# Folding the partition halves of the modulation sums on VectorE, and half as many matmuls to sum them on TensorE

## What is computed

```
mod_lat = (jax.nn.silu(c) @ w_mod[layer] + b_mod[layer])[:, None, :]
mod_ctx = (jax.nn.silu(c_ctx) @ w_mod[layer] + b_mod[layer])[None, None, :]
ml = jnp.split(mod_lat, N_MOD, axis=-1)
mc = jnp.split(mod_ctx, N_MOD, axis=-1)
x = x + 0.5 * ml[2] * swiglu(modulate(rms_norm(x, norm1_g[layer]), ml[0], ml[1]),
                              ffn1_w_in[layer], ffn1_w_out[layer])
```

## Time and profile before

| | |
|---|---|
| runs, median of 3 | 1243.94 us (1243.44 to 1244.24) |
| the profiled execution, span from the first to the last instruction | 1242.0 us |
| TensorE busy | 1226.1 us (99%), 7268 matmul passes |
| VectorE busy | 911.0 us (73%) |
| ScalarE busy | 591.5 us (48%) |
| GpSimd busy | 57.0 us (5%) |
| DMA | 214.22 MB, mean 172 GB/s |

### The profile page before, as it was taken

How to read it: one execution, slowest core, us unless ns; L and a number is a source line. 1 busy time by engine, 2 the same in 40 slices (tenths; PEclk the granted TensorE clock), 3 DMA queues, 4 the chain that set the end, 5 groups by cost and what they waited for, 6 DMA issues and landing times.

```text
span 1242.0 us, 19650 instructions
## 1 busy us (share of the span) xinstructions
PE 1226.1 (99%) x7268; PEld 1054.4 (85%) x7268; DVE 911.0 (73%) x1438; ACT 591.5 (48%) x917; POOL 57.0 (5%) x65
## 2 busy tenths in 40 slices
PE   8999999999999999999999999999999999999998
PEld 6788888888888798788888888889798999888887
DVE  3887877778657676788787776667769977667765
ACT  3632222222325546655555655546475576554552
POOL 2000000000002000000001000000012301000001
PEclk9999999999999999999999999999999999999999
DMA  9665544555422244323454565554533334455542
GB/s 387 233 241 203 203 169 172 201 203 199 145 73 94 102 170 169 136 102 106 167 202 170 188 227 194 189 183 167 208 135 116 123 133 173 170 182 208 185 170 102
DMA packets 31826, 214.22 MB, mean 172 GB/s; under 512 B 3472, under 2 KB 4752, under 8 KB 7056
## 3 DMA queue, kind: packets, MB, share of 16 engines
q1 hardware_dynamic: 31184, 211.83, 47.1%
q10 hardware_dynamic: 576, 1.48, 0.3%
HBM read 212.24 MB, written 1.05 MB: 172 GB/s over the span
## 4 chain that ended last, share of the span: by engine, by line
PE 91%; DVE 4%; DMA 2%; ACT 1%; issue 1%; SPq 0%; DVEq 0%; ACTq 0%
PE ps_u L1960 27%; PE ps_u L1969 14%; PE ps_u L1970 14%; PE ps_u L1971 14%; PE ps_u L1962 13%; DMA scr<-in_mods 1%; DVE w_lo L1081 1%; PE ps_a L1884 1%; PE ps_a L2219 1%; DMA raw<-in_stream 1%; PE ps_a L2203 1%; PE ps_a L1941 1%; PE ps_a L2413 0%; PE ps_a L1930 0%; ACT w_hi L553 0%
## 5 line engine op out<-in xcount | busy, mean ns | idle before, releaser
L553 ACT ACTIVATE w_hi<-raw 128x1024 fp32r<-128x1024 f32 x322 | 339.0, 1056 | 294.5 <-PE ps_u L1971 170.8
L1081 DVE TENSOR_TENSOR w_lo<-raw,w_hi 128x1024 fp32r<-128x1024 f32 x322 | 393.6, 1224 | 93.0 <-ACT w_hi L553 92.2
L1969 PE MATMUL ps_u<-x_hi,w_hi 128*128 128x512 f32 (+1 forms) x768 | 263.5, 343 | 2.8 <-DVE x_lo L1257 1.6
L1971 PE MATMUL ps_u<-x_hi,w_lo 128*128 128x512 f32 (+1 forms) x768 | 258.0, 336 | 0.0
L1960 PE MATMUL ps_u<-x_hi,w_hi 128*128 128x512 f32 x720 | 229.0, 399 | 0.4 <-DVE x_hi L1167 0.4
L1970 PE MATMUL ps_u<-x_lo,w_hi 128*128 128x512 f32 (+1 forms) x624 | 217.5, 349 | 0.0
L1969 PEld LDWEIGHTS ps_u<-x_hi,w_hi 128*128 128x128 f32 x768 | 145.6, 190 | 25.1 <-issue 6.9
L1962 PEld LDWEIGHTS ps_u<-x_hi,w_lo 128*128 128x128 f32 x720 | 135.2, 188 | 31.9
L1971 PEld LDWEIGHTS ps_u<-x_hi,w_lo 128*128 128x128 f32 x768 | 145.6, 190 | 15.3
L1962 PE MATMUL ps_u<-x_hi,w_lo 128*128 128x256 f32 x720 | 141.6, 278 | 0.0
L1960 PE MATMUL ps_u<-h_hi,w_hi 128*128 128x512 f32 x432 | 141.1, 396 | 0.0
(11 more groups left out here) (336 smaller groups left out, 1519.0 us busy)
## 6 DMA issues: line engine op xcount, KB each, us to landing
raw<-in_stream SPq DMA_DIRECT2D x153, 1024.0 KB, 4.8
wide_scr<-in_mods SPq DMA_DIRECT2D x18, 1024.0 KB, 7.0
scr<-in_mods SPq DMA_DIRECT2D x18, 1024.0 KB, 7.0
raw<-in_stream SPq DMA_DIRECT2D x8, 768.0 KB, 4.2
x<-in_tokens SPq DMA_DIRECT2D x2, 1024.0 KB, 6.5
wide_scr<-in_cmp_w SPq DMA_DIRECT2D x8, 256.0 KB, 5.1
sq<-in_cmp_w SPq DMA_DIRECT2D x2, 1024.0 KB, 6.1
out<-x SPq DMA_DIRECT2D x4, 256.0 KB, 2.2
```

Source lines behind the costliest of these rows:

```text
L553: act.activation(w_hi[:, k % 2, cols], raw[:, k % 2, cols], ACT.Copy).then_inc(h_ready, 1)
L1081: dve.tensor_tensor(w_lo[:, k % 2, cols], raw[:, k % 2, cols], w_hi[:, k % 2, cols].bitcast(F32), ALU.subtract).then_inc(l_ready, 1)
L1969: pe.matmul(dst, wh, xh, start=(kc == 0), stop=False)
L1971: ins = pe.matmul(dst, wl, xh, start=False, stop=(kc == span - 1))
```

## The change

`mod_sums` tiles are folded before TensorE sees them. Behind the last quarter of a chunk VectorE adds, for vector 0, partitions 64 to 127 of its tile to partitions 0 to 63, in place; then, when that is done, for vector 1 the halves of its tile, into partitions 64 to 127 of vector 0's tile. Each add counts the new semaphore `mod_folded`. `mod_sum` waits for two of them per chunk in place of the sixteen counts of `mod_added`, and takes that one tile with a new stationary operand `half_cols` (column 0 is ones on the lower half, column 1 on the upper): four matmuls in place of eight, none of them accumulating.

`half_cols` needs three more memsets on VectorE in front; `ones_ready` counts to 9 in place of 6. The two row-statistics semaphores of k and q become one (`head_rows`), so do their roots (`head_roots`) and q's reciprocal and scale (`q_scale_steps`); each wait stands where it stood.

```diff
+HALF_ROWS = P // 2
+        half_cols = sb("half_cols", [P, MOD_ROWS])
+        mod_folded = sem("mod_halves_folded")
...
-        kstat_rows = sem("kstat_rows_done")
+        head_rows = sem("k_then_q_stat_rows_done")
-        qstat_rows = sem("qstat_rows_done")
...
-            act.wait_ge(qstat_rows, 1)
+            act.wait_ge(head_rows, 2)
...
+            dve.memset(half_cols[:], 0.0).then_inc(ones_ready, 1)
             dve.memset(tick[:], 0.0).then_inc(o1_done, 1)
             dve.memset(vc_tok[:], 0.0).then_inc(ones_ready, 1)
-            dve.wait_ge(ones_ready, 4)
+            dve.wait_ge(ones_ready, 5)
+            for v in range(2):
+                dve.memset(half_cols[v * HALF_ROWS:(v + 1) * HALF_ROWS, v:v + 1], 1.0).then_inc(ones_ready, 1)
...
                         ins.then_inc(mod_added, 1)
+                if quarter == MOD_QUARTERS - 1:
+                    low, high = slice(0, HALF_ROWS), slice(HALF_ROWS, P)
+                    for v, rows in enumerate((low, high)):
+                        total_v = mod_sums[:, chunk % 2, v, :]
+                        dve.wait_ge(mod_added, 4 * n + 3 + v)
+                        if v:
+                            dve.wait_ge(mod_folded, 2 * chunk + 1)
+                        dve.tensor_tensor(mod_sums[rows, chunk % 2, 0, :], total_v[low, :], total_v[high, :], ALU.add)\
+                           .then_inc(mod_folded, 1)
...
             def mod_sum(c):
 
-                pe.wait_ge(mod_added, 4 * MOD_QUARTERS * (c + 1))
+                pe.wait_ge(mod_folded, 2 * (c + 1))
                 pe.wait_ge(mod_turned, c if c >= 3 else 2)
-                for v in range(2):
-                    for g in range(P // MOD_ROWS):
-                        rows = slice(g * MOD_ROWS, (g + 1) * MOD_ROWS)
-                        ins = pe.matmul(ps_a[rows, MOD_BANKS[c], 0:MOD_COLS], one_col[:, v, :],
-                                        mod_sums[:, c % 2, v, g * MOD_COLS:(g + 1) * MOD_COLS], start=(v == 0), stop=(v == 1))
+                for g in range(P // MOD_ROWS):
+                    rows = slice(g * MOD_ROWS, (g + 1) * MOD_ROWS)
+                    ins = pe.matmul(ps_a[rows, MOD_BANKS[c], 0:MOD_COLS], half_cols[:],
+                                    mod_sums[:, c % 2, 0, g * MOD_COLS:(g + 1) * MOD_COLS], start=True, stop=True)
                 ins.then_inc(mod_summed, 1)
...
-            pe.wait_ge(ones_ready, 6)
+            pe.wait_ge(ones_ready, 9)
```

More of the change, by code:

```diff
@@ L309, in program @@
         kstat_done = sem("kstat_done")
-        kroot_done = sem("kroot_done")
+        head_roots = sem("k_then_q_roots_done")
         krecip_done = sem("krecip_done")
@@ L321, in program @@
         qstat_done = sem("qstat_done")
-        qroot_done = sem("qroot_done")
-        qrecip_done = sem("qrecip_done")
-        q_scaled = sem("q_scale_ready")
+        q_scale_steps = sem("q_scale_steps")
         q_swapped = sem("q_swapped")
@@ L774, in _ @@
             act.wait_ge(kstat_done, 1)
-            act.activation(root[:, 0:8], ps_a[:, 1, 8:16], ACT.Sqrt, bias=eps, scale=1.0 / HD).then_inc(kroot_done, 1)
+            act.activation(root[:, 0:8], ps_a[:, 1, 8:16], ACT.Sqrt, bias=eps, scale=1.0 / HD).then_inc(head_roots, 1)
             with act.Fori(0, 2) as p:
@@ L805, in _ @@
             act.wait_ge(qstat_done, 1)
-            act.activation(root[:, 16:32], ps_a[:, 1, 16:32], ACT.Sqrt, bias=eps, scale=1.0 / HD).then_inc(qroot_done, 1)
+            act.activation(root[:, 16:32], ps_a[:, 1, 16:32], ACT.Sqrt, bias=eps, scale=1.0 / HD).then_inc(head_roots, 1)
             with act.Fori(2, 4) as p:
@@ L1437, in _ @@
             dve.drain().then_inc(drained, 1)
-            dve.wait_ge(kstat_rows, 1)
+            dve.wait_ge(head_rows, 1)
             dve.tensor_copy(k_stat_parts, ps_a[:, 1, S:NB]).then_inc(kstat_copied, 1)
@@ L1442, in _ @@
             split(0, k + 3, 1)
-            dve.wait_ge(kroot_done, 1)
+            dve.wait_ge(head_roots, 1)
             dve.reciprocal(rstd[:, 0:8], root[:, 0:8]).then_inc(krecip_done, 1)
@@ L1493, in _ @@
                     dve.tensor_tensor(q_rows[:, h, :], t1[:, j, 0:S], t1[:, j, S:NB], ALU.add).then_inc(drained, 1)
[L1496 to L1502, removed]
+            dve.wait_ge(head_roots, 2)
+            dve.reciprocal(rstd[:, 16:32], root[:, 16:32]).then_inc(q_scale_steps, 1)
+            dve.wait_ge(q_scale_steps, 1)
+            dve.tensor_scalar(q_scale[:], rstd[:, 16:32], float(HD) ** -0.5, None, ALU.mult).then_inc(q_scale_steps, 1)
+            dve.wait_ge(q_scale_steps, 2)
             def turned1(h, b=3):
@@ L2129, in _ @@
                                     start=True, stop=True)
-            ins.then_inc(kstat_rows, 1)
+            ins.then_inc(head_rows, 1)
             def k_stat(kc):
@@ L2152, in q_stat_rows @@
                                             start=(v == 0), stop=(v == 1))
-                    ins.then_inc(qstat_rows, 1)
+                    ins.then_inc(head_rows, 1)
             def q_stat(kc):
@@ L2192, in _ @@
                     gates(p, j)
-            pe.wait_ge(qroot_done, 1)
+            pe.wait_ge(head_roots, 2)
             pe.wait_ge(v_ready, 2)
```

## The result

The kernel after takes 1247.31 us (median of 15 runs, 1245.97 to 1248.93) beside 1244.2 us for the kernel before (15 runs, 1243.42 to 1244.48): a ratio of 1.0026, 95% interval 1.0019 to 1.0032. It is 3.1 us slower, a little past the 0.2% that can be told from no change. The prediction, 1245.5 us, has the sign and about half of the size (1.6 of 3.1 us); its range, 1243.0 to 1248.6, holds the time.

A forecast was written before the change was run, and what follows sets the result against it. TensorE, busy 99% of the span, was taken to bound the kernel. Waits of 4.66 us less 3.02 saved gave +1.64, so 1243.9 + 1.6 = 1245.5 us, range 1243.0 to 1248.6.

The forecast's parts named there:

- What is removed: TensorE's mod_sum: two sets of four passes fewer, 0.43 us per chunk, 3.0 us in all, all on the path.
- What is added: VectorE: two adds per chunk behind its last product, 1.22 us each, each starting 0.03 us after the instruction before.
- When TensorE gets its sums: Sums may begin 2.57 us after the products; TensorE waits in five of seven chunks, 4.66 us in all.
- The sum of the stage: First feed-forward stage: waits of 4.66 us less 3.02 saved, +1.64 us.
- The lateness is not carried on: VectorE's 2.6 us of lateness go into its idle time and cost nothing; the rival, +15 us, had chance 0.05.
- What lies around the span: The 1.9 us between the profiled span and the median of the runs was taken as unchanged.
- The rest at nothing: The three extra memsets in front, the merged k and q semaphores and TensorE's clock under new waits cost nothing.
- the forecast's own case: The whole kernel at 1244.4 to 1246.7 us, from bounds on the adds and the runs' spread; chance 0.78.
- the rival that the sums don't shrink: In mod_sum the switch between array shapes costs, not the sets: all 4.66 us of waits stay, 1248.6 us; chance 0.03.

The follow-up runs named there:

- one_wait: The changed kernel with the waits of a chunk's adds sorted, so the second add waits for the first add alone: 1247.17 us.
- folds_only: VectorE's two adds per chunk write into a spare tile that the sums don't read, TensorE keeps eight matmuls as in the kernel before: 1244.3 us.
- pe_only: The changed kernel without VectorE's adds, four matmuls per sum over vector 0's tile, so the sums lack the other vector: 1241.63 us.
- front_only: The kernel before with the three memsets and the unused tile half_cols in front, ones_ready counting to 9: 1244.93 us.
- late_sum: The changed kernel with mod_sum and the turning of its bank one unit later: 1242.44 us.
- After_again: The changed kernel run once more, same code: 1247.01 us.
- late_cols: The changed kernel with the memsets of half_cols moved from the front to behind the first normalisation: 1248.14 us.
- dve_pad: The kernel before with two tiny memsets of an unused tile per chunk on VectorE, with the adds' waits and one more: 1244.52 us.

## Why the prediction was right, and where it was not

Point by point, by its own steps:

- **What is removed:** 0.43 us per chunk predicted, 0.467 measured (3.27 in all for 3.02). The sets' price was right; missed was that the matmuls right behind the sums had run a little apart from each other.
- **What is added:** adds of 1.22 us predicted, 1.220 to 1.223 measured in all chunks, first add 0.03 behind the last product predicted, 0.031 to 0.032 measured. The two inputs in different halves make the add no longer (1.224 us for the subtraction in one place). The first add waits by its semaphore only for the product before the last, so it could have overlapped the last as the earlier trace rows show of a plain subtraction; it didn't, in seven of seven chunks. That agrees with the rule of the Trainium skill that the prediction cites ("VectorE: DVE Perf Modes", section "Two Vector instructions with no wait between them"). The second add's gap is mis-sized: 0.104 us in place of 0.03, and one_wait shows it to be the second wait of that add.
- **When TensorE gets its sums:** 2.57 us behind the products predicted, 2.63 in chunk 0 (87.04 to 89.67). From the passes before to the sums' first start, TensorE's waits come to 1.17, 0.93 and three of 0.94, 4.94 us in all, for 4.66 predicted; none in chunks 2 and 5, as predicted.
- **The sum of the stage:** 4.94 - 3.27 = 1.67 for +1.64. The two errors, each of about 0.3 us, cancel: the mechanism was right, and that its sum is right to 0.03 us is luck.
- **The lateness is not carried on:** right, shown by folds_only.
- **What lies around the span, "applied unchanged":** wrong by 0.34 us.
- **The rest at nothing:** wrong, and the larger part. The semaphores are nothing, as said, and the new waits don't lower TensorE's clock (1.00 from 40 to 380 us in after too). But the traces of kernels with the tile `half_cols` have a shift at 60 us of -0.03 to +1.30 us (nine of them, a mean of 0.54), those without it -0.09 to -0.03 (four besides before). And of the eight traces with four matmuls five lose 0.9 to 1.7 us between 850 us and the end, behind the late weight load, which is a mean over all eight of some 0.9. The prediction asked whether the memsets are waited for, but not what else they could move in front, nor what a shorter TensorE program moves outside its stage.
- **The range:** the forecast's own case, 1244.4 to 1246.7, doesn't hold the 1247.31. The range does, because it was drawn out to 1248.6 for the rival that the sums don't shrink, and pe_only shows that they do. So that the range holds is luck as well.

Together: 1.68 (stage) + 0.34 (around the span) + 0.54 (front) + 0.9 (weight load) = 3.5 us, beside 3.1 measured. The last two terms are means over single traces of different kernels, so this sum shows their order and no more. The change's own two traces have little of them (shifts of 0.22 and 0.34 at 60 us, 2.31 and 2.24 at the end), and their times, 1246.48 and 1246.41, lie 0.8 and 0.6 below the medians: what the median run loses beyond that stands in no trace of the change itself.

What makes the front late is TensorE's clock, about the time when the front's last modulation weights land (22.4 to 22.9 us where TensorE waits for them). Rows of 21 to 24 us (the granted clock is the third number from the right), and TensorE's timeline there: eight matmuls that only keep it busy (`ps_u<-ones`), then the last sums of the front. Before:

```profile
21.00:24.00 3.00, 2.46 (x29) 1.68 (x29) 1.54 (x2) 1.05 (x2) 0.00 (x0) 1.00 1.02 426
...
20.95 1.06 PE L2036 MATMUL ps_u<-ones 128*128 128x128 f32 x8
22.55 1.07 PE L1930 MATMUL ps_a<-scr,sc_pad 128*32 128x256 f32 x16 [0.55 <-DMA scr<-in_mods]
```

front_only, which is 1.00 us late at 60 us:

```profile
21.00:24.00 3.00, 3.00 (x20) 2.45 (x22) 1.22 (x1) 1.18 (x2) 0.00 (x0) 0.51 1.01 421
...
21.43 1.91 PE L2041 MATMUL ps_u<-ones 128*128 128x128 f32 x8
23.28 1.36 PE L1935 MATMUL ps_a<-scr,sc_pad 128*32 128x256 f32 x16
```

late_sum, which is not late:

```profile
21.00:24.00 3.00, 2.80 (x32) 2.02 (x32) 1.53 (x2) 1.05 (x2) 0.00 (x0) 1.00 1.03 429
...
21.30 1.06 PE L2047 MATMUL ps_u<-ones 128*128 128x128 f32 x8
22.56 1.07 PE L1942 MATMUL ps_a<-scr,sc_pad 128*32 128x256 f32 x16 [0.20 <-DMA scr<-in_mods]
```

A granted clock of 1.00 is the upper level of 2.4 GHz, and 0.51 means that the lower one of 1.2 GHz held for nearly all of the stretch. In before and late_sum the clock is back by 21 us, and TensorE is idle when the weights land; in front_only the eight matmuls take 1.91 us in place of 1.06, and the sums start late and end 1.0 us late. In before and front_only alike the clock falls at 17.1 us, while TensorE waits for a load (1.17 us until 17.57, 1.29 until 17.70); it is back at 20.6 us in the one and at 23.9 in the other.

The fourteen traces go together: in the five without the tile and in late_sum the clock is back by 21.8 us and the shift lies between -0.09 and 0; in the other eight it is back at 22.1 to 28.5 us and the shift is 0.22 to 1.30. After_again, the first of the eight, is the exception: there the weights themselves land 0.39 us later. The mean clock of a timed run points the same way in one_wait: 1245.34 to 1246.07 us in the four runs at 0.998 to 1.000, 1247.09 to 1248.21 in the seven at 0.995 and 0.996. And before isn't free of it: of its 92 runs in the three groups, the five above 1245.5 us have 0.995 or 0.996, where the median is 0.997. In after's own runs the mean clock doesn't sort the times. Why the lower level lasts longer in nearly every kernel with the tile stays open; the memsets' place doesn't decide it (late_cols has a shift of 0.40).

## What to carry to other kernels

Work that is moved from the bounding engine to one with room must be finished when the bounding engine asks: here five of seven waits ate more than the saving, on an engine 75% busy, and asking one unit later turned +1.68 us in the stage into -3.27. Before folding, look at the slack of every hand-over, and count the waits on the last dependent instruction (one fewer gave 0.07 us each time). And a change of a fraction of a per cent is not its stage alone: the kernels with 28 matmuls fewer lost some 0.9 us of the 3.27 saved, in the mean of eight traces, behind a load that had little room; and a lower clock in front cost up to 1.3 us where matmuls that only keep the engine busy stood ahead of those that count.

The sums one unit later are the fastest kernel that was run and still sums both vectors (1242.44 and 1242.59 us). The same with the sorted waits, which might save the 0.34 us around the span too, was not tried.

## What the runs showed of the hardware that was not expected

- A second wait on an instruction that depends on the one before it adds 0.07 us to the gap (0.104 for 0.034 us), as an instruction of 21 ns of its own. That the first add waits for the last product in place of the one before it changes next to nothing (0.035 for 0.031 us). Dve_pad's extra waits, whose counts are reached early, run beside the products (at 85.58 and 85.68 us, the memset behind them at 86.69).
- The time around the span is 1.80 or 2.15 us with a scatter of 0.02 to 0.04 us (2.01 with 0.12 in dve_pad), and changes with VectorE's list of instructions: seven waits fewer bring it from 2.15 to 1.80.
- Instruction packets (16 KB, one about every 25 us in the modulation stage) move with the length of TensorE's program. A 768 KB weight load whose first packets follow 0.8 to 1.0 us behind the start of one took 4.1 to 5.7 us, and in four of the five traces where it took over 4.9 us the 1 MB load behind it took 7.5 to 8.0 us in place of 4.7 to 4.9.
- At the lower clock the sixteen passes of the front's sums take 1.93 us (one_wait at 22.42 us), at the upper one 1.07.
